# Sample maxima, exponentials and turned probabilities of a woven attention, in halves over several slots

## The chip, the cores and the metric

One Trainium2 chip, one core. The metric is the device time of one execution in microseconds (us), the median of the runs. A profile is one further execution with the hardware profiler on; times in it count from the start of its span.

## The reference, cut to what matters

One decoder layer is run for a prompt of 1024 tokens and for 8 sample sequences ("batches") of 4 new tokens each, which also attend to 4096 past tokens in a paged cache of keys and values (32 pages of 128 tokens for each batch, 8 heads of 64). After the attention come cross attention and a layer of 32 experts. The part that matters here:

```python
sp = jnp.einsum('bqhd,bkhd->bhqk', q, k_past) * scale + d_new[:, :, :, None] + rev[:, :, None, :]
sn = jnp.einsum('bqhd,bkhd->bhqk', q, k) * scale + d_new[:, :, :, None] - d_new[:, :, None, :]
p = jax.nn.softmax(jnp.concatenate([sp, where(causal, sn, -inf)], axis=-1), axis=-1)
out = p[..., :n_past] @ v_past + p[..., n_past:] @ v
```

So for each batch a score over all 4096 past tokens and the 4 new ones, its maximum, the exponentials, and the weighing of the values. The prompt has the same kind of attention among its own 1024 tokens.

## The kernel before

The attention of the samples and that of the prompt are woven into one list of 74 **slots** (n = 0 to 73; NSU = 64, LAG = 10, SU = 8 slots for a batch). Every engine walks the same list in its own loop (PE L1306, ACT L1908, DVE L2375) and they meet through semaphores, so the order within a slot is written out by hand for each engine. A slot n of the samples stands for 4 pages.

- **Keys.** SP loads 4 pages of keys (1 MB) into one of two buffers `kraw` (L928). It may refill a half of a buffer only when DVE has turned the keys that lay in it. DVE turns the keys of slot n + 2 in slot n (`turn_keys`, L2222, two transposes, L2230).
- **Scores.** PE makes the scores of slot n (L1270), ACT copies them out (`copy_scores`), PE sorts those of slot n - 1 (L1279), and DVE adds the decay `rev`, writes them into `sprob` of the batch and keeps a running maximum (`join_scores`, L2339).
- **The batch's softmax.** When the 8 slots of batch b are joined, which is in slot 8(b + 1), DVE finishes the maximum over the four page groups (L2351, L2354, eight small reduces inside `join_scores`) and signals `s_max`. ACT's `exp_pages` (L1888), last in ACT's slot 8(b + 1), takes the exponentials of both halves of `sprob` and of the new scores. In slot 8(b + 1) + 1 DVE's `turn_sample_probs` (L2357) turns all 1024 columns into `sprobT` (L2363) and the new ones into `pnewT` (L2364), and signals `st_ready`. There is one `sprobT` for all batches, so DVE first waits until PE has used up the batch before (`v_used`), the last of whose pages PE weighs at the end of that very slot 8(b + 1) + 1.
- **Values.** PE weighs the 4 pages of values of slot n - 10 at the end of slot n (`weigh_pages`, L1282, matmuls L1290; the batch's last page is followed by its new tokens, L1294). After a batch's last page DVE masks and sums the result (`mask_own`, L2366). POOL loads the values (`load_values`, L871, DMA at L876) into two buffers. The last ten loads (n = 54 to 63) also use places that the attention has done with (L258): place 4 is free when the last scores are joined, and place 5, which is the memory of the two `sprob`, when `st_ready` says that all of them are turned (L869). The odd ones of these ten are issued by SP (L994), in this order in its queue: values 55, 57, 59 (place 5), 61, the weights `c0` of the next stage (2 MB), values 63, and then the transformed input `xnT` from `xn_d` (L1000, 2 MB), without which the next stage's matmuls (L1338) don't start.
- **The prompt.** From slot 29 to 71 each slot holds one or two half units of the prompt's attention: PE's scores of the next unit (L1218, L1224), DVE's `biased` (L2301, with the maximum, L2312 and L2317), ACT's `exp_prompt` (L1880), PE's turning of the probabilities (L1232), ACT's copies of them (`probT`, L1830), PE's weighing (L1245) and the sums through `diag` (DVE L2328, PE L1249). Up to slot 28 there are projections of the prompt in their place (L1167, L1182).
- `spread_queries` (L2213, L2217) lays out the queries of the next batch; DVE does it in slot 8k ahead of everything but `join_scores`. PE needs it in slot 8(k + 1).

DVE's order in a slot is: `join_scores` of n - 1 (with the end of the maximum), `spread_queries`, the prompt's work, `turn_sample_probs`, `turn_keys`, `mask_own`. Below, "slot 8k" is one with n divisible by 8; slots 8k to 8k + 3 are called the four behind a batch's end, the other four the quiet ones.

Of the kernel before, what the change touches and what calls it, by code (L numbers as in the profile page):

```python
# [18 lines left out]
ALU = mybir.AluOpType  # L19
ACT = mybir.ActivationFunctionType  # L20
AX = mybir.AxisListType.X
# [6 lines left out]
DB, DS = 8, 4  # L28
# [8 lines left out]
QH = DS * H  # L37
# [108 lines left out]
def build_program(nc, t):  # L146

    ctx = ExitStack()
    with ctx:
# [100 lines left out]
        SU = PAGES // 4  # L250
# [608 lines left out]
        def values_free(eng, n):  # L859

            place = value_place(n)
            if values_in(n):
                eng.wait_ge(v_used, max(m for m in range(n) if value_place(m) == place) + 1)
            elif place in (2, 3):
                eng.wait_ge(kt_ready, 2 * (NSU - 3 + place))
            elif place == 4:
                R.read(eng, "sp", NSU - 1)
            elif place == 5:
                eng.wait_ge(st_ready, DB)  # L869

        def load_values(eng, n):  # L871

# [260 lines left out]
        def _(pe):  # L1133
# [148 lines left out]
            def weigh_pages(n):  # L1282

                b, u = n // SU, n % SU
                pe.wait_ge(v_in[value_place(n)], 64 * values_in(n) + 64)
                pe.wait_ge(st_ready, b + 1)
                if u == 0:
                    R.pe_free(pe, "so", b)
                for j in range(4):
                    last = nc.tensor.matmul(bank(6)[j * QH:(j + 1) * QH, :], sprobT[:, u, j * QH:(j + 1) * QH],  # L1290
                                            vpage[value_place(n)][:, j, :], start=u == 0, stop=u == SU - 1 and j > 0)
                last.then_inc(v_used, 1)
                if u == SU - 1:
                    nc.tensor.matmul(bank(6)[0:QH, :], pnewT[b % 2], vtok[0:NS, PT, :], start=False, stop=True  # L1294
                                     ).then_inc(R.full, 1)
# [531 lines left out]
        def _(act):  # L1827
# [57 lines left out]
                    copy(("pt", k, p, g), probT[p][:, j0:j0 + nj, :],  # L1885
                         lambda b: b[:, 0:nj * P].rearrange("p (j x) -> p j x", j=nj))

            def exp_pages(b):  # L1888
                act.wait_ge(s_max, b + 1)
                act.wait_ge(side_ready, SNEW_READY)  # L1890
                for r in range(2):
                    x = sprob[b % 2][:, r * 512:(r + 1) * 512]
                    nc.scalar.activation(x, x, ACT.Exp, bias=negmax[:, b:b + 1], accum_out=sums[:, b, r:r + 1]
                                         ).then_inc(s_exp, 1)
                nc.scalar.activation(pnew[b % 2], snew[:, b, :], ACT.Exp, bias=negmax[0:QH, b:b + 1],
                                     accum_out=sums[0:QH, b, 2:3]).then_inc(s_exp, 1)

# [10 lines left out]
            for n in range(NSU + LAG):  # L1908
                if n < NSU:
                    copy_scores(n)  # L1910
                if n == PROMPT0 - 1:
                    exp_prompt(0, 0)
                for k, p in halves(n):
                    if p == 0:
                        exp_prompt(k, 1)
                    copy_turned(k, p)
                    if p == 1 and k + 1 < NU:
                        exp_prompt(k + 1, 0)
                for item in items(n):
                    copy_item(*item)  # L1920
                if KOUT0 <= n < KOUT0 + TILES:
                    copy_key_rows(n - KOUT0)
                if SU <= n < NSU + SU and n % SU == 0:
                    exp_pages(n // SU - 1)
            def keep_first(name, f, q, after, kept=kept_c):

                if after is not None:
# [235 lines left out]
        def _(dve):  # L2163
# [49 lines left out]
            def spread_queries(b):  # L2213

                for g in range(4):
                    rows = slice(g * 32, (g + 1) * 32)
                    nc.vector.tensor_copy(  # L2217
                        qblk[b % 2].rearrange("p e (x q g) -> p e x q g", x=3, g=4)[rows, :, 0:3:2, :, g],
                        qgrp[rows, :, :, :, b * DS:(b + 1) * DS].rearrange("p j e x q -> p (j e) x q"))
                dve.drain()  # L2220

            def turn_keys(n):  # L2222

                if n >= NSU:
                    return
                dve.wait_ge(k_in[n % 2], 64 * (n // 2 + 1))
                if n >= 2:
                    R.made(dve, "sq", n - 2)
                for x in range(2):
                    nc.vector.transpose(kt[n % 2].rearrange("p c e s -> p (c e s)")[:, x * 1024:(x + 1) * 1024],  # L2230
                                        kraw[n % 2].rearrange("p c d -> p (c d)")[:, x * 1024:(x + 1) * 1024]
                                        ).then_inc(kt_ready, 1)
# [51 lines left out]
            def take_new():  # L2284

                dve.wait_ge(neg_stored, 32)
                nc.vector.tensor_tensor(nbias, consts[0:QH, C_MASK:C_MASK + DB * NS].rearrange("p (b s) -> p b s", b=DB),
                                        nd.unsqueeze(1).to_broadcast([QH, DB, NS]), ALU.add)
                dve.drain()
                R.made(dve, "snew")  # L2290
                nc.vector.tensor_tensor(snew, bank(R.bank("snew"))[0:QH, 0:DB * NS].rearrange("p (b s) -> p b s", b=DB), nbias,
                                        ALU.add).then_inc(R.by["dve"], 1)
                dve.drain()
                nc.vector.tensor_reduce(tops[0:QH, :, SU:SU + 1], snew, AX, ALU.max).then_inc(side_ready, 1)
                R.made(dve, "lf")
                b = bank(R.bank("lf"))
                nc.vector.tensor_copy(lfo[:, 0:PT, :], b[:, 0:PT * H].rearrange("p (i h) -> p i h", i=PT))
                nc.vector.tensor_copy(lfo[0:NS, PT, :], b[0:NS, PT * H:TILES * H]).then_inc(R.by["dve"], 1)
                dve.drain()
# [39 lines left out]
            def join_scores(n):  # L2339

                b, u = n // SU, n % SU
                if u == 0:
                    dve.wait_ge(rev_in[b % 2], 16 * (b // 2 + 1))
                R.made(dve, "sp", n)
                nc.vector.tensor_tensor_reduce(out=sprob[b % 2][:, u * PAGE:(u + 1) * PAGE], in0=bank(3)[:, 0:PAGE],
                                               in1=rev[b % 2][:, u * PAGE:(u + 1) * PAGE], scale=1.0, scalar=-3e38,
                                               op0=ALU.add, op1=ALU.max, accum_out=tops[:, b, u:u + 1]).then_inc(R.by["dve"], 1)
                if u == SU - 1:
                    dve.drain()
                    for g in range(4):  # L2350
                        nc.vector.tensor_reduce(crest[:, g:g + 1], tops[g * QH:(g + 1) * QH, b, :], AX, ALU.max)  # L2351
                    dve.drain()
                    for g in range(4):
                        last = nc.vector.tensor_reduce(negmax[g * QH:(g + 1) * QH, b:b + 1], crest, AX, ALU.max, negate=True)  # L2354
                    last.then_inc(s_max, 1)

            def turn_sample_probs(b):  # L2357

                dve.wait_ge(s_exp, 3 * b + 3)
                if b:  # L2360
                    dve.wait_ge(v_used, b * SU)
                flat = sprobT.rearrange("p u x -> p (u x)")
                nc.vector.transpose(flat, sprob[b % 2])  # L2363
                nc.vector.transpose(pnewT[b % 2], pnew[b % 2]).then_inc(st_ready, 1)  # L2364

            def mask_own(b):  # L2366

# [7 lines left out]
            for n in range(NSU + LAG):  # L2375
                if 0 < n <= NSU:
                    join_scores(n - 1)
                if n % SU == 0 and n + SU < NSU:
                    spread_queries(n // SU + 1)
                if n == PROMPT0 - 1:  # L2380
                    biased(0, 0)
                if n == END:
                    take_prompt(NU - 1)
                if n < 3:
                    take_forget(n)
                for k, p in halves(n):
                    if p == 0 and k:
                        take_prompt(k - 1)
                    if k + 1 < NU and p < len(chunks(k + 1)):
                        biased(k + 1, p)  # L2390
                    if p == 1:
                        invert_sums(k)
                if n == 5:
                    take_new()
                if SU < n < NSU + SU and n % SU == 1:
                    turn_sample_probs(n // SU - 1)
                turn_keys(n + 2)
                if 2 * SU < n < NSU + LAG - 1 and n % SU == 1:
                    mask_own(n // SU - 2)
            near, far = slice(0, HT), slice(HT, NT)  # L2400
# [919 lines left out]
```

## Time and profile before

| what | value |
|---|---|
| median of 3 runs | 2012.65 us (2010.44 to 2016.42) |
| the profiled execution: its own time, its span | 2018.6 us, 2016.9 us |
| busy: PE, DVE, ACT, POOL | 1876.5, 861.9, 440.3, 249.4 us |
| DMA | 458.57 MB, mean 227 GB/s |
| chain that ended last | PE 82%, DVE 6%, ACT 4%, DMA 4%, issue 3% |
| slots 0 to 28 | 70.9 to 273.0 us |
| slots 29 to 73 | 273.0 to 547.2 us, then the next stage |

How to read it: PE is the busiest engine, but it is busy through matmuls that wait on others in some stages. The woven attention is the part of the span from 71 to 547 us. What a change in it is worth is what it moves the instant at which the next stage's first matmul (L1338) starts.

### The profile page before, as it was taken

Reading aid. Unit: us, or ns where it says so; the run is one execution under the profiler, and the core shown is the slowest. Engines: PE = TensorE matmul, PEld = TensorE weight load, DVE = VectorE, ACT = ScalarE, POOL = GpSimd, SP = SyncE. Lnnn points to the kernel's source line nnn. Section 1 sums busy time; section 2 is a strip of 40 time slices with the busy share of each in tenths; the row PEclk is TensorE's granted clock in tenths of the full one; section 3 lists DMA queues with packets and bytes.
Section 4 is the critical chain, followed back from the end, with each engine's and each line's share of the span. In section 5 each row is a group of like instructions: output and inputs, shape, how many; then the busy total and the mean of one; then the engine's idle time right before and its main releaser. Section 6 shows DMA issues by size and latency. Waiting matters only on the chain.

```text
span 2016.9 us, 33708 instructions
## 1 busy us (share of the span) xinstructions
PE 1876.5 (93%) x12473; PEld 1121.2 (56%) x12473; DVE 861.9 (43%) x1921; ACT 440.3 (22%) x1017; POOL 249.4 (12%) x381
## 2 busy tenths in 40 slices
PE   6999998888999999999999998987999999999994
PEld 4677655555488868888874487444333333333331
DVE  5644467777656523333344647245111111111115
ACT  3111124444301011101110305131222222212213
POOL 0203333333100000000000000000111111111110
PEclk9999999999999999999999999996999999999997
DMA  7859999999911140210121205344999999999966
GB/s 255 277 169 343 354 337 364 352 339 347 331 63 65 44 154 11 63 53 11 55 74 63 87 1 183 121 171 177 372 381 382 374 373 376 371 372 374 371 222 264
DMA packets 208164, 458.57 MB, mean 227 GB/s; under 512 B 18721, under 2 KB 47418, under 8 KB 207618
## 3 DMA queue, kind: packets, MB, share of 16 engines
q1 hardware_dynamic: 177554, 365.30, 50.8%
q0 software_dynamic: 30448, 91.13, 12.8%
q8 instruction: 100, 1.64, 0.3%
q14 instruction: 62, 0.51, 0.1%
HBM read 432.44 MB, written 32.17 MB: 230 GB/s over the span
## 4 chain that ended last, share of the span: by engine, by line
PE 82%; DVE 6%; ACT 4%; DMA 4%; issue 3%; DVEq 1%; SPq 0%; ACTq 0%; POOLq 0%; POOL 0%
PE ps L1338 20%; PE ps L1691 11%; PE ps L1722 6%; PE ps L1167 6%; PE ps L1403 6%; PE ps L1702 6%; PE ps L1432 5%; PE ps L1731 3%; PE ps L1182 3%; PE ps L1544 2%; PE ps L1290 2%; PE ps L1270 2%; PE ps L1148 1%; DVE kt L2230 1%; DMA vpage<-in_cache_v 1%
## 5 line engine op out<-in xcount | busy, mean ns | idle before, releaser
L1691 PE MATMUL ps<-gu,xgT 128*64 128x512 f32 x1024 | 228.7, 599 | 0.6 <-ACT xgT L2046 0.6
L1338 PE MATMUL ps<-xnT,ring 128*128 128x264 f32 x768 | 184.5, 392 | 3.2 <-ACT xnT L741 1.9
L2230 DVE STREAM_TRANSPOSE kt<-kraw 128x1024 f32<-128x1024 f32 x128 | 151.1, 1219 | 34.5 <-DMA kraw<-in_cache_k 25.3
L1338 PEld LDWEIGHTS ps<-xnT,ring 128*128 128x128 f32 x768 | 147.8, 193 | 30.5 <-ACT xnT L741 2.2
L876 POOL DMA_DIRECT2D vpage<-in_cache_v x228 | 122.4, 537 | 291.6 <-PE ps L1290 233.6
L3053 DVE TENSOR_TENSOR sig_a<-ps,sig_a 128x256 f32<-128x256 f32 x32 | 13.6, 425 | 322.9 <-ACT sig_a L2050 322.9
L1691 PEld LDWEIGHTS ps<-gu,xgT 128*64 128x64 f32 x1024 | 71.1, 138 | 133.0 <-issue 130.2
L1722 PE MATMUL ps<-wd,hidT_a 128*64 128x512 f32 x512 | 116.9, 598 | 20.2 <-ACT hidT_a L2056 11.2
L1702 PE MATMUL ps<-gu,xgT 128*32 128x512 f32 x1024 | 115.8, 592 | 0.0
L1167 PE MATMUL ps<-xnT,early 128*128 128x352 f32 x320 | 101.2, 472 | 4.4 <-DVE xnT L2174 4.4
L1167 PEld LDWEIGHTS ps<-xnT,early 128*128 128x128 f32 x320 | 60.6, 194 | 38.2 <-issue 8.7
L1270 PEld LDWEIGHTS ps<-kt,qblk 128*32 128x32 f32 x2048 | 58.2, 112 | 40.6 <-issue 37.9
L1722 PEld LDWEIGHTS ps<-wd,hidT_a 128*64 128x64 f32 x512 | 37.2, 136 | 77.7 <-issue 60.6
L1955 ACT ACTIVATE gate<-gate 128x264 f32<-128x264 f32 x64 | 27.0, 423 | 234.8 <-DVE gate L2599 234.8
L3187 POOL DMA_DIRECT2D x_d<-xs x5 | 2.7, 539 | 599.4 <-DVE xs L756 599.4
L1702 PEld LDWEIGHTS ps<-gu,xgT 128*32 128x32 f32 x1024 | 33.1, 110 | 77.0 <-issue 77.0
L1290 PE MATMUL ps<-vpage,sprobT 128*32 128x512 f32 x480 | 66.4, 625 | 7.4 <-DMA vpage<-in_cache_v 7.4
L1270 PE MATMUL ps<-kt,qblk 128*32 128x128 f32 x2048 | 69.9, 277 | 0.9 <-DVE kt L2230 0.9
L1182 PE MATMUL ps<-early,xnT 128*128 128x256 f32 (+1 forms) x288 | 66.0, 384 | 0.0
L2590 DVE TENSOR_TENSOR gate<-ps,gate 128x264 f32<-128x264 f32 x64 | 27.7, 433 | 82.9 <-PE ps L1403 82.9
L1731 PE MATMUL ps<-wd,hidT_b 128*32 128x512 f32 x512 | 61.6, 598 | 1.3 <-ACT hidT_b L2065 1.3
L1403 PE MATMUL ps<-cyT,upw 128*128 128x264 f32 x256 | 62.2, 386 | 0.0
(482 smaller groups left out, 2945.9 us busy)
## 6 DMA issues: line engine op xcount, KB each, us to landing
kraw<-in_cache_k SPq DMA_DIRECT2D x256, 256.0 KB, 5.3
wd<-in_w_expert_down SPq DMA_DIRECT2D x31, 2048.0 KB, 21.5
gu<-in_w_expert_gate SPq DMA_DIRECT2D x30, 2048.0 KB, 20.3
gu<-in_w_expert_up SPq DMA_DIRECT2D x30, 2048.0 KB, 25.1
vpage<-in_cache_v POOLq DMA_DIRECT2D x228, 256.0 KB, 5.8
ring<-in_w_in SPq DMA_DIRECT2D x12, 1024.0 KB, 8.1
yy<-y_d SPq DMA_DIRECT2D x16, 512.0 KB, 10.4
early<-in_w_in SPq DMA_DIRECT2D x6, 1024.0 KB, 11.7
```

Of the source, the lines that this page charges most:

```text
L876: eng.dma_start(vpage[value_place(n)][:, p, :], t["cache_v"][ds(page, 1)].rearrange("a s d -> (a s) d")).then_inc(v_in[value_place(n)], 16)
L1167: last = nc.tensor.matmul(bank(R.bank(name, f, n))[:, 0:NC_], weight[:, k, :], xnT[:, k, cols_of(n)], start=k == 0, stop=k == KD - 1)
L1182: last = nc.tensor.matmul(bank(R.bank(kind, a, b))[0:r, 0:256], xnT[:, k, b * P:b * P + r], early[a][:, k, :], start=k == 0, stop=k == KD - 1)
L1270: last = nc.tensor.matmul(bank(5)[j * 32:(j + 1) * 32, 0:PAGE], qblk[b % 2][:, 2 * j + x % 2, first:first + 32], kt[n % 2][:, :, 4 * j + x ...
L1290: last = nc.tensor.matmul(bank(6)[j * QH:(j + 1) * QH, :], sprobT[:, u, j * QH:(j + 1) * QH], vpage[value_place(n)][:, j, :], start=u == 0 ...
L1338: last = nc.tensor.matmul(bank(R.bank(name, f, q))[:, 0:QT], weight[:, k], src[:, k, cols], start=k == 0, stop=k == HK - 1)
L1403: last = nc.tensor.matmul(bank(R.bank(name, f, q, half))[:, 0:QT], upw[f % 2][:, x, k, :], src[:, k, quarter(half, q)], start=k == 0, stop ...
L1691: last = nc.tensor.matmul(bank(0)[h * BA:(h + 1) * BA, :].rearrange("p (x n) -> p x n", x=2), src[:, k, 0:BA], weight[:, k, :, h * DE // 2 ...
L1702: last = nc.tensor.matmul(bank(1)[c:c + BB, :].rearrange("p (x n) -> p x n", x=2), src[:, k + odd, BA:BLK], weight[:, k + odd, :, h * DE / ...
L1722: last = nc.tensor.matmul(bank(6)[o * BA:(o + 1) * BA, :], hidT_a[:, c % 2, c // 2 * BA:(c // 2 + 1) * BA], weight[:, c, o * 512:(o + 1) * ...
L1731: last = nc.tensor.matmul(bank(7)[q:q + BB, :], hidT_b[:, odd, c // 2 * BB:(c // 2 + 1) * BB], weight[:, c + odd, o * 512:(o + 1) * 512], ...
L2230: nc.vector.transpose(kt[n % 2].rearrange("p c e s -> p (c e s)")[:, x * 1024:(x + 1) * 1024], kraw[n % 2].rearrange("p c d -> p (c d)")[: ...
```

## The change

The end of the maximum becomes a step of its own (`join_tops`) and is put behind the prompt's work in slot 8k. ACT takes the exponentials of the first half of `sprob` in slot 8k and those of the second half and of the new scores in slot 8k + 1. DVE turns the first half in slot 8k + 1, behind `turn_keys`, waiting for PE to be through with only the first four pages' places of the batch before, and the second half with `pnewT` in slot 8k + 3. `st_ready` counts halves, PE's weighing and the load into place 5 wait on the new counts. `spread_queries` goes to the end of slot 8k + 4.

```diff
--- before.py
+++ after.py
@@ -866,7 +866,7 @@
             elif place == 4:
                 R.read(eng, "sp", NSU - 1)
             elif place == 5:
-                eng.wait_ge(st_ready, DB)
+                eng.wait_ge(st_ready, 2 * DB)
 
         def load_values(eng, n):
 
@@ -1283,7 +1283,7 @@
 
                 b, u = n // SU, n % SU
                 pe.wait_ge(v_in[value_place(n)], 64 * values_in(n) + 64)
-                pe.wait_ge(st_ready, b + 1)
+                pe.wait_ge(st_ready, 2 * b + 1 + u // (SU // 2))
                 if u == 0:
                     R.pe_free(pe, "so", b)
                 for j in range(4):
@@ -1885,13 +1885,14 @@
                     copy(("pt", k, p, g), probT[p][:, j0:j0 + nj, :],
                          lambda b: b[:, 0:nj * P].rearrange("p (j x) -> p j x", j=nj))
 
-            def exp_pages(b):
+            def exp_pages(b, r):
                 act.wait_ge(s_max, b + 1)
+                x = sprob[b % 2][:, r * 512:(r + 1) * 512]
+                nc.scalar.activation(x, x, ACT.Exp, bias=negmax[:, b:b + 1], accum_out=sums[:, b, r:r + 1]
+                                     ).then_inc(s_exp, 1)
+
+            def exp_new(b):
                 act.wait_ge(side_ready, SNEW_READY)
-                for r in range(2):
-                    x = sprob[b % 2][:, r * 512:(r + 1) * 512]
-                    nc.scalar.activation(x, x, ACT.Exp, bias=negmax[:, b:b + 1], accum_out=sums[:, b, r:r + 1]
-                                         ).then_inc(s_exp, 1)
                 nc.scalar.activation(pnew[b % 2], snew[:, b, :], ACT.Exp, bias=negmax[0:QH, b:b + 1],
                                      accum_out=sums[0:QH, b, 2:3]).then_inc(s_exp, 1)
 
@@ -1921,7 +1922,9 @@
                 if KOUT0 <= n < KOUT0 + TILES:
                     copy_key_rows(n - KOUT0)
                 if SU <= n < NSU + SU and n % SU == 0:
-                    exp_pages(n // SU - 1)
+                    exp_pages(n // SU - 1, 0)
+                if SU <= n < NSU + SU and n % SU == 1:
+                    exp_pages(n // SU - 1, 1), exp_new(n // SU - 1)
             def keep_first(name, f, q, after, kept=kept_c):
 
                 if after is not None:
@@ -2345,23 +2348,27 @@
                 nc.vector.tensor_tensor_reduce(out=sprob[b % 2][:, u * PAGE:(u + 1) * PAGE], in0=bank(3)[:, 0:PAGE],
                                                in1=rev[b % 2][:, u * PAGE:(u + 1) * PAGE], scale=1.0, scalar=-3e38,
                                                op0=ALU.add, op1=ALU.max, accum_out=tops[:, b, u:u + 1]).then_inc(R.by["dve"], 1)
-                if u == SU - 1:
-                    dve.drain()
-                    for g in range(4):
-                        nc.vector.tensor_reduce(crest[:, g:g + 1], tops[g * QH:(g + 1) * QH, b, :], AX, ALU.max)
-                    dve.drain()
-                    for g in range(4):
-                        last = nc.vector.tensor_reduce(negmax[g * QH:(g + 1) * QH, b:b + 1], crest, AX, ALU.max, negate=True)
-                    last.then_inc(s_max, 1)
-
-            def turn_sample_probs(b):
-
-                dve.wait_ge(s_exp, 3 * b + 3)
+
+            def join_tops(b):
+
+                dve.drain()
+                for g in range(4):
+                    nc.vector.tensor_reduce(crest[:, g:g + 1], tops[g * QH:(g + 1) * QH, b, :], AX, ALU.max)
+                dve.drain()
+                for g in range(4):
+                    last = nc.vector.tensor_reduce(negmax[g * QH:(g + 1) * QH, b:b + 1], crest, AX, ALU.max, negate=True)
+                last.then_inc(s_max, 1)
+
+            def turn_sample_probs(b, r):
+
+                dve.wait_ge(s_exp, 3 * b + (1, 3)[r])
                 if b:
-                    dve.wait_ge(v_used, b * SU)
-                flat = sprobT.rearrange("p u x -> p (u x)")
-                nc.vector.transpose(flat, sprob[b % 2])
-                nc.vector.transpose(pnewT[b % 2], pnew[b % 2]).then_inc(st_ready, 1)
+                    dve.wait_ge(v_used, b * SU - (SU // 2, 0)[r])
+                half = slice(r * 512, (r + 1) * 512)
+                last = nc.vector.transpose(sprobT.rearrange("p u x -> p (u x)")[:, half], sprob[b % 2][:, half])
+                if r == 1:
+                    last = nc.vector.transpose(pnewT[b % 2], pnew[b % 2])
+                last.then_inc(st_ready, 1)
 
             def mask_own(b):
 
@@ -2375,8 +2382,6 @@
             for n in range(NSU + LAG):
                 if 0 < n <= NSU:
                     join_scores(n - 1)
-                if n % SU == 0 and n + SU < NSU:
-                    spread_queries(n // SU + 1)
                 if n == PROMPT0 - 1:
                     biased(0, 0)
                 if n == END:
@@ -2392,9 +2397,15 @@
                         invert_sums(k)
                 if n == 5:
                     take_new()
+                if 0 < n <= NSU and n % SU == 0:
+                    join_tops(n // SU - 1)
+                turn_keys(n + 2)
                 if SU < n < NSU + SU and n % SU == 1:
-                    turn_sample_probs(n // SU - 1)
-                turn_keys(n + 2)
+                    turn_sample_probs(n // SU - 1, 0)
+                if SU < n < NSU + SU and n % SU == 3:
+                    turn_sample_probs(n // SU - 1, 1)
+                if n % SU == 4 and n + SU < NSU:
+                    spread_queries(n // SU + 1)
                 if 2 * SU < n < NSU + LAG - 1 and n % SU == 1:
                     mask_own(n // SU - 2)
             near, far = slice(0, HT), slice(HT, NT)
```

## Rows read from the trace of the kernel before

**Rows 1.** Stretch: us, busy PE, PEld, DVE, ACT, POOL, clock, DMA share, GB/s

```profile
157.00:268.00 111.00, 110.35 (x1096) 71.96 (x1094) 54.51 (x100) 14.95 (x46) 36.53 (x68) 1.00 1.00 354
```

**Rows 2.** The same view, slots 32 to 63 in stretches of four slots

```profile
294.77:326.35 31.58, 26.10 (x331) 15.93 (x327) 24.97 (x72) 14.44 (x35) 10.72 (x20) 0.95 0.94 328
326.35:350.92 24.57, 21.88 (x326) 14.64 (x322) 16.82 (x50) 10.36 (x28) 10.69 (x20) 1.00 1.02 373
350.92:381.11 30.19, 23.98 (x312) 13.98 (x307) 25.80 (x73) 12.38 (x31) 8.60 (x16) 0.94 0.99 363
381.11:404.07 22.96, 21.71 (x321) 14.07 (x317) 16.66 (x49) 9.94 (x25) 8.59 (x16) 1.00 0.97 341
404.07:432.65 28.58, 24.00 (x302) 14.02 (x298) 23.92 (x72) 11.20 (x31) 8.59 (x16) 0.88 0.90 309
432.65:458.22 25.57, 22.46 (x325) 14.18 (x321) 17.67 (x49) 9.72 (x25) 8.58 (x16) 1.00 1.03 378
458.22:484.03 25.81, 22.15 (x319) 13.75 (x314) 22.89 (x70) 11.85 (x31) 8.58 (x16) 1.00 0.97 334
484.03:507.55 23.52, 20.99 (x309) 13.34 (x305) 15.33 (x46) 8.97 (x25) 9.33 (x18) 1.00 1.00 365
```

**Rows 3.** DVE in order of time, slots 48 and 49

```profile
406.59 0.64 DVE L2351 TENSOR_REDUCE crest<-tops 32x1 f32<-32x9 f32 x4
...
407.98 0.93 DVE L2217 COPY qblk<-qgrp 32x64 f32<-32x64 f32 x4
409.02 0.29 DVE L2312 CUSTOM_DVE_ANT_0 prob<-ps,negk 128x128 f32<-128x128 f32 x1
...
416.39 1.25 DVE L2363 STREAM_TRANSPOSE sprobT<-sprob 128x1024 f32<-128x1024 f32 x1 [1.64 <-PE ps L1290]
```

**Rows 4.** Lines L2363 and L2364: durations min/median/max ns, first and last start; idle before

```profile
L2363 DVE STREAM_TRANSPOSE sprobT<-sprob x8: 1245/1246/1246, 148.1 to 517.7; 128x1024 f32<-128x1024 f32 x8
...
  PE ps L1290: 19.7, 7
...
L2364 DVE STREAM_TRANSPOSE pnewT<-pnew x8: 156/156/157, 149.3 to 518.9; 32x32 f32<-32x32 f32 x8
```

**Rows 5.** ACT in order of time, around the exponentials in slot 32

```profile
302.35 0.71 ACT L1893 ACTIVATE sprob<-sprob,negmax 128x512 f32<-128x512 f32 x1
...
304.22 1.03 ACT L1880 ACTIVATE prob<-prob,fstat 128x896 f32<-128x896 f32 x1
```

**Rows 6.** PE in order of time: some of its waits of slots 30 to 65

```profile
289.91 1.97 PE L1245 MATMUL ps<-probT,vtok 128*64 128x128 f32 x32 [0.94 <-ACT probT L1830]
...
301.48 0.44 PE L1249 MATMUL ps<-diag,onesw 128*64 128x128 f32 x4 [1.03 <-DVE diag L2328]
...
305.96 1.73 PE L1232 MATMUL ps<-consts,prob 128*128 128x128 f32 x7 [2.21 <-ACT probT L1830]
...
515.62 0.96 PE L1232 MATMUL ps<-consts,prob 128*128 128x128 f32 x7 [1.22 <-ACT probT L1830]
```

**Rows 7.** Waits of SP's queue from 500 to 560 us: total, times, longest

```profile
SPq L876 <- DVE pnewT L2364: 6.4, 1, 6.4
```

**Rows 8.** SP's queue in order of time, end of the attention

```profile
508.50 12.60 SPq L876 DMA_DIRECT2D vpage<-in_cache_v  x8
523.51 1.88 SPq L876 DMA_DIRECT2D kraw<-in_cache_v  x4
525.44 1.44 SPq L825 DMA_DIRECT2D ring<-in_w_in  x2
529.27 2.56 SPq L876 DMA_DIRECT2D vpage<-in_cache_v  x4
536.16 0.81 SPq L1000 DMA_DIRECT2D xnT<-xn_d  x2
```

**Rows 9.** In order of time: DVE in slot 67, PE at the attention's end

```profile
528.66 0.15 DVE L2317 TENSOR_REDUCE fstat<-ftop 128x2 f32<-128x2 f32 x1
...
544.92 1.04 PE L1294 MATMUL ps<-vtok,pnewT 32*32 32x512 f32 x2
547.21 2.03 PE L1338 MATMUL ps<-xnT,ring 128*128 128x264 f32 x6 [1.25 <-DMA xnT<-xn_d]
```

## The prediction

> **What bounds the kernel now.** I read the stretches first, because the page's shares mix stages. From 157 to 268 us, slots 11 to 27, PE is busy for 110.4 of 111.0 us [rows 1]. Up to there DVE and ACT may wait as they like; PE does not. So the change can give nothing ahead of slot 29, and the edits in those slots cost nothing either, as long as PE's 100% covers them. If that cover were gone, DVE's wait for PE's last page there (part of the 19.7 us of rows 4) would be the first to show.
>
> From slot 29 on it is different. The reader should see in rows 2 that the stretches come in two kinds. The four slots behind a batch's end (first, third, fifth and seventh row) take 31.6, 30.2, 28.6 and 25.8 us, together 116.2. The four quiet ones take 24.6, 23.0, 25.6 and 23.5, together 96.6. The difference is 19.5 us, of which 1.0 each is work (the new tokens' matmul, one such as the 1.04 us of L1294 in rows 9); 15.5 us is what batch ends cost on top. In the same stretches the clock that PE was granted sinks to 0.95, 0.94, 0.88 and the DMA rate is 334 GB/s (38.8 MB in 116.2 us) against 365 (35.2 MB in 96.6 us). No engine is full there. The bound is the round between PE, ACT and DVE for each prompt unit, with the transfers close behind it.
>
> **Part 1, DVE's order in slot 8k.** Today the eight reduces (0.64 us for four of them, so 1.3) and `spread_queries` (0.93) stand ahead of `biased`: it starts at 409.02, and could at 406.6 [rows 3]. That is 2.3 us off the way from the prompt's scores to their maximum, to ACT's exponential and to `diag`. Price of it on PE: the wait for `diag` in slot 33 is 1.03 us [rows 6], and is the largest of three in slots 8k + 1 (the others 0.2 and 0.7). I take 1.9 us in all. What is late next: `s_max`, now behind `invert_sums`. ACT reaches the exponentials only after its copies and the next unit's exponential, about 1.5 to 3 us after the prompt's maximum, so I cost it at nothing; without that cover it is 1.3 us in each of five slots.
>
> **Part 2, ACT.** The block of exponentials occupies ACT from 302.35 to 304.2 [rows 5], and `exp_prompt` of the next half unit stands behind it. Halved, 0.7 us stays in slot 8k and about 1.0 goes to the end of slot 8k + 1, where ACT has nothing queued until PE's next scores. PE waits for ACT's `probT` once in each slot 8k + 1: five waits, the first 2.21 and the last 1.22 us, together 8.8 [rows 6]. Such a wait in a quiet slot is 0.94 [rows 6], since the turning of a half unit with two groups always waits for a copy. The parts 1 and 2 together take these five down to that: 8.8 - 5 x 0.9 = 4.3 us.
>
> **Part 3, DVE's wait for PE.** DVE stands 19.7 us, in seven waits, for the batch before to be used up [rows 4], and `turn_keys`, `mask_own` and the next slot's joins are queued behind it. The new waits ask for pages that were weighed three slots earlier, so they are free. `mask_own` still waits for the same instant, but with neither L2363's 1.25 us nor the keys left behind it. As a gain on PE it is already in the 4.3 us, and it lets keys be refilled some us earlier, which raises the DMA rate in the slow stretches.
>
> **Part 4, the transposes.** One of 1024 columns is 1.25 us, one of 32 is 0.16 [rows 4]; on that line 512 columns are 0.68. Two are 0.12 us more than the one, at least 0 and at most 1.25 (two full ones). They and `spread_queries` now lie in slots 8k + 3 and 8k + 4, which were quiet: 0.8 and 0.9 us of DVE. DVE is busy for 17 of 25 us there; I charge a quarter, 0.3 us on each of four, 1.2 us.
>
> **Part 5, the clock.** One minus the clock, times the length, is 1.6, 1.8 and 3.4 us in the slow stretches [rows 2]: 6.8 us of PE's work lost, each right behind PE's longest waits. With waits of 0.9 I expect half of it back where PE paces, and take 2.0; ends 0 and 6.8. Sum of the middle: 1.9 + 4.3 + 2.0 - 1.2 = **7 us gained**, against 15.5 at the very most.
>
> A check by bytes: if the slow stretches ran at the quiet ones' 365 GB/s, their 38.8 MB would take 106.2 us, 10 us less. So 7 is not barred by the transfers as rows 2 show them. The Trainium skill, DMA: Bandwidth & Descriptors, section Specifications, gives a limit of about 358 GB/s for one core on the memory. By it the 74 MB of slots 32 to 63 need 206.7 of their 212.8 us, and the gain could be 6 us at most. The trace disagrees: 373 and 378 GB/s over some 25 us each [rows 2].
>
> **Part 6, the end: a wait that grows.** Place 5 of the values is the memory of `sprob`, and its load (values 59) now waits for the second half of the last batch, turned in slot 67 and not in 65. SP already waits 6.4 us for `pnewT` [rows 7], which is ready at 519.0 [rows 4]. In slot 67 the prompt's maximum is done at 528.8 [rows 9], then 0.68 and 0.16 us of transposes: ready at 529.6, **10.6 us later** (DVE idles behind it, so they cost DVE nothing). In SP's queue stand, behind this load, values 61, the weights `c0`, values 63 and `xnT`. From 519.0 to the end of the issue of values 63 at 531.8 SP takes 12.8 us [rows 8]; now that ends at 542.4. `xnT` was issued at 536.16 [rows 8], because it waited for the prompt's last scores, so 4.3 us of the delay are hidden and 6.2 are not. It lands 11 us after its issue, and PE waits for exactly that landing (547.21, [rows 9]). Values 59 are weighed at about 536, which a load issued at 529.6 to 531.6 just reaches; values 63 come late, but inside the wait for `xnT`. Ends: the landing may take fewer than 11 us; alone, 2.2 MB at 375 GB/s are 6 us, which leaves 1 us; the other end is 10.6. By bytes: from 529.6 on six megabytes of values and weights and 2.2 of `xnT`, 8.5 MB at 365 GB/s, end at 552.8, 5.6 us late. I take **5.5 us lost**.
>
> **Sum.** -7 + 5.5 = -1.5; everything behind 547 us only shifts. Against the profiled execution's own 2018.6 that is 2017.1. It lies 6.0 us above the median of the runs, 2012.65, so the forecast in runs is 2011.1. A measurement can tell about 0.3% (6 us) here, so this is "no change".
>
> **Rivals.**
> Rival 1, faster: the batch ends give most of what they hold, 12 of the 15.5 us (the keys are refilled earlier, the clock stays up), and the end costs 2, since `xnT` lands on idle DMA engines. Then -10, 2002.6. For it: DVE's 19.7 us of waiting, the full 10 us by bytes. Against it: the DMA share is 0.94 to 1.02 in most of rows 2. Chance 0.28.
> Rival 2, slower: one mechanism, SP's queue at the end. The price is up to the full 10.6 us if values 59 and 61 are late for their own slots and `c0` for DVE's sums of it, with `xnT` behind them. It decides from the point where the second half is ready more than 4.3 us after 519.0. With 3 us gained before it: +7.6, 2020.2. For it: rows 7 and 8, PE has only 1.25 us of idle time before `xnT` lands. Against it: latency falls when the queues are empty. Chance 0.17.
> Rival 3, the pages are the bound: slots 32 to 63 can't run faster than the 354 GB/s that rows 1 hold for 111 us. 74 MB are then 209 us, a gain of 3.7, less the end's 5.5: +1.8, 2014.5. The page on DMA named above would be its rule. Chance 0.15.
> The change not doing what it says: DVE waits at `mask_own` as it did at the transpose. That falls under rival 3's time.
>
> **Numbers.** Forecast 0.40, rivals 0.28, 0.17, 0.15. Faster by over 0.3%: most of rival 1 and a sixth of the forecast, 0.32. Slower: most of rival 2 and a little of the others, 0.19. The rest, 0.49, is the same. The range goes from rival 1 to rival 2, 2001 to 2021; the forecast's own is 2006 to 2016.
>
> **What would show it.** Right: no wait of DVE for L1290 ahead of L2363; the stretches of slots 32 to 35, 40 to 43 and 48 to 51 shorter by some 2 us each with the clock near 1.00; ACT's block halved; SP's wait for `pnewT` up from 6.4 to some 17 us; `xnT` issued later than the prompt's last scores and PE idle for over 5 us before L1338. Wrong: PE idle before L1338 still about 1 us; the four-slot stretches unchanged; ACT waiting for `s_max`; or PE waiting for values 59.

## The result, and the profile after

The changed kernel is slower: a median of 2023.2 us (2017.0 to 2026.7, 14 runs) against 2013.4 for the kernel before (2009.8 to 2019.9, 14 runs) in the same series. The ratio is 1.0039, 95% interval 1.0029 to 1.0050, so 5.8 to 10.1 us. The forecast was 1.5 us faster, with 2021 us as the upper end.

First the stretches of four slots in the changed kernel, the counterpart of [rows 2], then its last stretch, from slot 64 to the first matmul of the next stage. The columns are those of [rows 1].

```profile
291.66:327.53 35.87, 27.36 (x334) 16.25 (x330) 25.07 (x69) 14.58 (x35) 10.76 (x20) 0.86 0.91 336
327.53:351.60 24.07, 21.75 (x329) 14.60 (x325) 16.48 (x52) 10.33 (x28) 10.76 (x20) 1.00 0.95 330
351.60:379.50 27.90, 23.64 (x313) 14.30 (x309) 23.65 (x69) 12.62 (x31) 8.62 (x16) 0.94 1.01 376
379.50:403.10 23.60, 21.74 (x325) 14.11 (x321) 19.64 (x56) 9.95 (x25) 8.63 (x16) 1.00 0.98 360
403.10:430.20 27.10, 22.55 (x302) 13.72 (x298) 23.08 (x68) 11.55 (x31) 8.61 (x16) 0.94 1.01 374
430.20:453.50 23.30, 21.94 (x325) 14.29 (x321) 18.18 (x55) 9.61 (x25) 8.61 (x16) 1.00 1.00 363
453.50:478.30 24.80, 21.76 (x322) 13.50 (x317) 22.22 (x69) 12.22 (x31) 8.61 (x16) 1.00 0.95 340
...
502.98:550.94 47.96, 37.03 (x318) 17.43 (x310) 26.07 (x90) 17.80 (x43) 6.46 (x12) 0.91 0.78 279
```

From slot 40 on the stretches behind a batch's end are 1.0 to 2.3 us shorter each, as forecast; in the second profile of the same kernel (after_again) the one of slots 40 to 43 is not, with 31.7 us. The first one is 4.3 us longer. And the last one lasts 48.0 us where the kernel before takes 39.7. The same columns for that stretch in the kernel before, then for its two parts in the changed kernel, up to the issue of values 59 and from there on:

```profile
507.55:547.21 39.66, 34.98 (x318) 17.51 (x311) 22.81 (x84) 17.68 (x43) 7.84 (x15) 1.00 0.99 344
```

```profile
502.98:524.70 21.72, 19.04 (x172) 9.56 (x167) 14.35 (x58) 11.34 (x28) 4.30 (x8) 1.00 0.53 196
524.70:550.94 26.24, 18.00 (x151) 7.87 (x150) 11.72 (x33) 6.47 (x16) 2.15 (x4) 0.83 0.98 347
```

In the first part the DMA engines are busy for about half of the time (0.53). SP's queue in order of time shows why; the rows answer to [rows 8] and [rows 7].

```profile
503.93 1.90 SPq L876 DMA_DIRECT2D vpage<-in_cache_v  x4
524.72 1.89 SPq L876 DMA_DIRECT2D vpage<-in_cache_v  x4
529.01 2.00 SPq L876 DMA_DIRECT2D kraw<-in_cache_v  x4
531.05 1.45 SPq L825 DMA_DIRECT2D ring<-in_w_in  x2
534.91 3.57 SPq L876 DMA_DIRECT2D vpage<-in_cache_v  x4
538.58 0.86 SPq L1000 DMA_DIRECT2D xnT<-xn_d  x2
```

```profile
SPq L876 <- DVE pnewT L2370: 16.5, 1, 16.5
```

Values 57 go out at 503.9, then SP stands 16.5 us (before: 6.4) until the last batch's second half is turned; values 59 follow at 524.7. PE in order of time, the counterpart of [rows 9]:

```profile
538.82 1.06 PE L1290 MATMUL ps<-vpage,sprobT 128*32 128x512 f32 x8
545.80 1.94 PE L1290 MATMUL ps<-vpage,sprobT 128*32 128x512 f32 x8 [5.91 <-DMA vpage<-in_cache_v]
547.66 1.91 PE L1294 MATMUL ps<-vtok,pnewT 32*32 32x512 f32 x2
550.94 9.71 PE L1338 MATMUL ps<-xnT,ring 128*128 128x264 f32 x32 [1.37 <-DMA xnT<-xn_d]
```

PE idles 5.9 us for values 63 and 1.4 for `xnT`, and right after the idle time the same eight matmuls take 1.94 us instead of 1.06: the granted clock is 0.60 on the mean from 539.9 to 550.9 us.

A second profile of the kernel before showed how far one profile may be trusted, so I compare durations within the span, of all profiles taken. Each ratio is to the kernel before in the same series; a version had 12 runs there (the changed kernel 14 in its first series, the last two of the table 6). All in us, from PE's first score matmul of slot 29, its sort of slot 64 and its first L1338:

```
kernel            slots 29-63   64 to next stage   ratio to before, 95% interval
before               234.5          39.7            -
before_again         233.1          39.5            (one run)
gate_alone           232.0          47.9            1.0040  1.0025-1.0054
before_c0            232.8          39.5            1.0004  0.9992-1.0016
bias_later_only      236.8          40.2            1.0002  0.9987-1.0016
changed kernel       231.4          48.0            1.0039  1.0029-1.0050
after_again          231.2          48.1            1.0031  1.0016-1.0045
last_whole           229.9          39.9            0.9996  0.9983-1.0009
c0_ahead             228.2          43.0            1.0000  0.9988-1.0012
both_ends            234.2          40.3            0.9994  0.9982-1.0006
tops_ahead           233.9          38.7            0.9985  0.9970-1.0001
keys_ahead           226.5          39.8            0.9971  0.9958-0.9984
keys_tops_behind     229.7          40.7            0.9992  0.9978-1.0006
keys_bias            227.7          40.2            0.9973  0.9959-0.9986
bias_later           230.4          39.0            0.9982  0.9968-0.9997
bias_later_tops      225.9          39.1            0.9953  0.9937-0.9969
best_again           226.6          39.1            0.9953  0.9936-0.9970
```

Kernels with the middle of before (first five rows) take 233.8 us on the mean for slots 29 to 63, those with the changed middle (next five) 231.0. With a scatter of about 2 us from profile to profile the 2.8 are uncertain by more than 1 us. The end is 8.4 us longer and hardly scatters. So -2.8 + 8.4 = +5.6 us, to be held against the 6.2 and 7.9 of the two series.

### The profile page after: what moved, and what is told of

Read it like the earlier page. It is cut to its first block, busy times and chain, and to the rows that moved or that the text cites. A ratio compares the mean times of both kernels' runs of the same rounds, so it can differ in the third digit from the quotient of the medians.

```text
span 2018.1 us, 33715 instructions
## 1 busy us (share of the span) xinstructions
PE 1872.8 (93%) x12473; PEld 1119.7 (55%) x12473; DVE 861.5 (43%) x1929; ACT 442.1 (22%) x1017; POOL 250.3 (12%) x381
## 4 chain that ended last, share of the span: by engine, by line
PE 81%; DVE 5%; DMA 4%; issue 4%; ACT 3%; DVEq 1%; SPq 1%; POOLq 0%; POOL 0%; ACTq 0%
PE ps L1338 20%; PE ps L1691 11%; PE ps L1722 6%; PE ps L1167 6%; PE ps L1403 6%; PE ps L1702 6%; PE ps L1432 5%; PE ps L1182 3%; PE ps L1731 3%; PE ps L1544 3%; PE ps L1270 2%; PE ps L1290 2%; DMA vpage<-in_cache_v 2%; PE ps L1148 1%; PE ps L1218 1%
## 5 line engine op out<-in xcount | busy, mean ns | idle before, releaser
L1338 PE MATMUL ps<-xnT,ring 128*128 128x264 f32 x768 | 183.4, 390 | 3.3 <-ACT xnT L741 1.9
L1338 PEld LDWEIGHTS ps<-xnT,ring 128*128 128x128 f32 x768 | 147.1, 192 | 31.1 <-DMA xnT<-xn_d 3.1
L1830 ACT ACTIVATE probT<-ps 128x512 f32<-128x512 f32 (+3 forms) x96 | 43.7, 488 | 85.9 <-PE ps L1232 85.9
```

Of the source, the lines that this page charges most:

```text
L1338: last = nc.tensor.matmul(bank(R.bank(name, f, q))[:, 0:QT], weight[:, k], src[:, k, cols], start=k == 0, stop=k == HK - 1)
```

## The experiments

### The end

**The changed kernel again** (after_again), no edit.

> The changed kernel once more, for a second profile and a second timing. Theory Q (the queue at the end: the load into place 5 waits for the second half, and the input of the next stage stands behind it): 6 to 10 us over the kernel before; SP's wait for pnewT 15 to 20 us, PE idle 5 to 8 us in all before L1338. Rival M (the middle: DVE stands longer at the keys in slots 29 to 63, as for the 5.6 us in slot 35 of the first profile): the same total, but slot 64 is reached no earlier than the 507.6 us of the kernel before. Rival K (no gain anywhere, the early slots lose): slot 29 later than 273 us.

1.0031; SP waits 16.5 us for `pnewT`, PE waits 5.5 us for values 63 and 1.4 for `xnT`. Theory Q's picture to the row. Slot 64 came at 503.5, so rival M doesn't hold the loss; slot 29 came at 272.2, so K doesn't either.

**The last batch turned whole** (last_whole).

```diff
-                if SU <= n < NSU + SU and n % SU == 1:
+                if n == NSU or (SU <= n < NSU and n % SU == 1):
                     exp_pages(n // SU - 1, 1), exp_new(n // SU - 1)
...
-                if SU < n < NSU + SU and n % SU == 3:
+                if n == NSU + 1 or (SU < n < NSU and n % SU == 3):
                     turn_sample_probs(n // SU - 1, 1)
```

> The changed kernel, with the last batch's two halves both exponentiated in slot 64 and turned in slot 65, so that the load into place 5 is free as early as before. Theory Q: 7 to 9 us faster than the changed kernel, so 0 to 5 us faster than the kernel before; PE idle before L1338 back to 1 to 2 us. Rival M: within 2 us of the changed kernel, since the middle is untouched. Rival K: the same as M.

0.9996: 7 us come back from one batch of eight. SP waits 6.5 us for `pnewT`, the end takes 39.9 us.

**The delay alone, in the kernel before** (gate_alone).

```diff
             elif place == 5:
                 eng.wait_ge(st_ready, DB)
+                R.read(eng, "ps", NU - 2, 0, 1)
```

> The kernel before, unchanged but for one more wait: SP's load into place 5 also waits for DVE's maximum of the half unit in slot 67, about 9.5 us later than pnewT. The delay alone. Theory Q: 6 to 9 us slower than the kernel before, with 5 to 8 us of PE idle time before L1338. Rival M: 0 to 2 us slower.

1.0040. One wait on SP, nothing else, costs as much as the whole change. PE in order of time in that kernel (one line further down in the file):

```profile
547.63 1.94 PE L1291 MATMUL ps<-vpage,sprobT 128*32 128x512 f32 x8 [5.62 <-DMA vpage<-in_cache_v]
549.50 1.91 PE L1295 MATMUL ps<-vtok,pnewT 32*32 32x512 f32 x2
552.78 7.47 PE L1339 MATMUL ps<-xnT,ring 128*128 128x264 f32 x20 [1.37 <-DMA xnT<-xn_d]
```

Counted from slot 64, these are the rows of the changed kernel to 0.1 us, and PE's wait for values 63 to 0.3. The price of the end is shown from both sides: taken away in last_whole, and put in here alone.

**c0 ahead of values 59** (c0_ahead; in the kernel before, before_c0; with last_whole, both_ends).

```diff
-                if n == NSU - 3:
+                if n == NSU - 7:
                     ring_load(sp, "c0")
```

> The changed kernel, with the 2 MB of weights c0 issued ahead of values 59 (behind values 57), so that they move while SP would stand. The wait of SP for the second half stays. Theory Q with the price in bytes behind the wait (8.5 MB less 2.1): 4 to 6 us faster than the changed kernel. Theory Q with the price in SP's issues alone: some 1.5 us faster (the issue of c0 is 1.4 us). Rival M: within 1 us of the changed kernel.

1.0000, and the end takes 43.0 us: five of the eight are back, more than the 1.4 us of issue. `xnT` goes out 3.0 us earlier, since the issue of values 63 is also short again (1.9 us, not 3.6), and it lands 10.4 us after its issue, not 12.4. So SP's own time for c0 is the smaller part of the five; the rest is that fewer bytes are left to move behind the wait. That the short issue comes from that too is likely, not shown. Of the eight us, what is left is a wait of 4.4 us for `xnT`, issued 32.6 us behind the start of slot 64 (28.6 in the kernel before).

> The kernel before, with the weights c0 issued ahead of values 59. There SP stands only 6.4 us for pnewT. Theory Q: the end is bound by what stands in SP's queue and by bytes, so 1 to 4 us faster than the kernel before, since xnT lands earlier and PE's wait ahead of L1338 (1.25 us) goes. Rival E (PE's own work ends the attention there): within 1 us. Slot 64 as in the other profile of before: 506 to 508 us under theory S, 502 to 504 under rival T.

> The changed kernel with the last batch turned whole in slot 65 and with c0 ahead of values 59. Theory S with Q: 4 to 7 us faster than the kernel before, no PE wait of over 1 us ahead of L1338. Rival T: as before_c0, so 1 to 4 us faster than the kernel before.

1.0004 and 0.9994. Where SP isn't stopped for long, c0's place is worth nothing. The wait ahead of L1338 did vanish in before_c0, but sixteen matmuls later, at 548.2, PE waits 0.3 us for `xnT` all the same, and the end takes 39.5 us, as in the kernel before (39.5 and 39.7). My 1 to 4 us were wrong, rival E was right.

**The kernel before, a second profile** (before_again).

> The kernel before, for a second profile of its middle: its first profile was of a run 4 to 5 us above its median. Theory S (the change gains 4 us in slots 29 to 63 and loses 8 behind them): slot 64 is reached at 506 to 508 us, as in the first profile (507.6), against 503 in the changed kernel's two. Rival T (the middle gains nothing, the first profile of before was a slow one): 502 to 504 us.

Slot 64 came at 505.3, between the two theories. The other profiles of that middle gave 504.5 to 508.8, of the changed one 499.3 to 506.5. The changed middle probably gains something, but less than my first pair of profiles said.

### The middle

**Maxima and queries back ahead of the prompt** (tops_ahead: last_whole with `join_tops` and `spread_queries` where the kernel before has them).

> As last_whole, but with the end of the maximum and the layout of the next queries back ahead of the prompt's work in slot 8k: what is left of the change is the halved exponentials, the halved transposes and the keys ahead of them. If part 1 of the prediction (2.3 us off the prompt's way) is worth its 1.9 us: 1 to 3 us slower than last_whole, and PE waits for diag L2328's counterpart by 0.2 to 1 us in slots 33, 49 and 57. Rival (the transfers take back what the middle gives): within 1 us of last_whole.

0.9985, 0.1% faster than last_whole, not slower. PE's waits for `diag` did come back, with 1.0 and 0.9 us in slots 33 and 49, so the gain forecast by part 1 is there, and something else in the move costs as much. Alone the intervals overlap. So the end of the maximum was moved by itself.

**The keys first, nothing else** (keys_ahead), and that with the end of the maximum behind the prompt's work (keys_tops_behind).

```diff
+                turn_keys(n + 2)
                 if SU < n < NSU + SU and n % SU == 1:
                     turn_sample_probs(n // SU - 1)
-                turn_keys(n + 2)
```

> The kernel before, with only DVE's turn_keys put ahead of the turning of the sample's probabilities in slots 8k + 1: no halves, maxima and queries as they were. If the gain of tops_ahead comes from the keys no longer standing behind DVE's wait for PE: 1 to 4 us faster than the kernel before and the late keys near 310 us show up here too. If it comes from the halved exponentials: within 1 us of the kernel before, and no such wait.

> keys_ahead with only the end of the maximum moved behind the prompt's work of slot 8k. The prediction's part 1: 1 to 3 us faster than keys_ahead, so 0.9955 to 0.9967 of the kernel before. Theory P (that move is what spoils last_whole against tops_ahead): 2 to 5 us slower than keys_ahead, so 0.998 to 1.0.

0.9971 and 0.9992: two lines swapped in the kernel before give 6 us, and the moved maximum takes 4 of them back (the two intervals overlap by 0.0006; last_whole against tops_ahead and bias_later against bias_later_tops point the same way). The two come from different series, each against its own kernel before. Of the late keys near 310 us a wait of 1.2 us shows up in keys_ahead; PE's 2 us waits for ACT in slots 8k + 1 are still there; that they give the transfers their time is my reading, and wasn't tried. In the waits of keys_tops_behind from 200 to 530 us (total, times, longest), and in ACT's order of time in slot 48, stands a wait that the kernel before doesn't have:

```profile
ACT sprob L1893 <- DVE negmax L2357: 4.6, 5, 1.2
```

```profile
404.15 0.83 ACT L1880 ACTIVATE prob<-prob,fstat 128x640 f32<-128x640 f32 x1 [1.22 <-DVE fstat L2317]
...
406.23 0.72 ACT L1893 ACTIVATE sprob<-sprob,negmax 128x512 f32<-128x512 f32 x1 [1.16 <-DVE negmax L2357]
```

ACT gets the prompt's maximum 1.0 us earlier, counted from the start of slot 49, and then stands 1.16 us at the sample's. That alone is 0.2 to 0.3 us. But PE's wait for `probT` in the slot behind is 2.83 us there and 1.95 in keys_ahead, and its matmuls behind the longer wait run slower. PE in slot 49 of keys_tops_behind:

```profile
409.65 1.01 PE L1232 MATMUL ps<-consts,prob 128*128 128x128 f32 x5 [2.83 <-ACT probT L1830]
410.59 1.94 PE L1290 MATMUL ps<-vpage,sprobT 128*32 128x512 f32 x8
```

In keys_ahead the same groups take 0.74 and 1.07 us, and slot 49 as a whole 8.9 us instead of 10.8. The columns of [rows 1] for slots 29 to 63, keys_ahead first, then keys_tops_behind:

```profile
272.63:499.13 226.50, 195.08 (x2748) 122.47 (x2744) 177.98 (x512) 97.54 (x253) 81.00 (x152) 0.99 0.99 359
```

```profile
272.14:501.88 229.74, 200.03 (x2749) 124.73 (x2745) 178.06 (x512) 98.01 (x253) 82.08 (x153) 0.96 0.98 356
```

The granted clock is 0.96 instead of 0.99, and PE is busy 5 us longer with the same matmuls. Between these two profiles the clock lost behind longer waits of PE covers the 3.2 us of difference; another such wait is for values at the end of slot 40, 3.7 us against 2.4. It isn't the whole account: keys_bias, which also has the maximum in its old place, takes 227.7 us at 0.97. The changed kernel has the same wait of ACT for `negmax`, four times in its slots 29 to 63:

```profile
ACT sprob L1891 <- DVE negmax L2359: 3.5, 4, 1.2
```

**The late keys.** In the changed kernel DVE, in order of time in slot 34, and PE in slot 35:

```profile
309.16 0.69 DVE L2315 CUSTOM_DVE_ANT_0 prob<-ps,negk 128x512 f32<-128x512 f32 x1
...
316.42 2.37 DVE L2233 STREAM_TRANSPOSE kt<-kraw 128x1024 f32<-128x1024 f32 x2 [6.56 <-DMA kraw<-in_cache_k]
...
320.07 0.48 DVE L2331 TENSOR_SCALAR diag<-consts,fstat 128x128 f32<-128x128 f32 x2
```

```profile
314.14 0.88 PE L1245 MATMUL ps<-probT,vtok 128*64 128x128 f32 x12 [0.63 <-ACT probT L1830]
320.61 0.70 PE L1249 MATMUL ps<-diag,onesw 128*64 128x128 f32 x4 [5.59 <-DVE diag L2331]
```

The whole prompt work of slot 35 is queued behind the keys. The stretches of the changed kernel around it, in the columns of [rows 1]:

```profile
300.00:318.00 18.00, 12.89 (x173) 7.95 (x173) 10.47 (x27) 6.35 (x17) 5.86 (x11) 0.96 1.03 397
318.00:330.00 12.00, 8.66 (x74) 4.78 (x74) 8.54 (x28) 4.34 (x10) 1.41 (x3) 0.63 0.70 227
```

In the first the DMA engines move 397 GB/s (353 in the first profile of the kernel before in the same stretch, 363 to 391 in three others of that middle), and the keys, issued up to 301.0, need 15 us; in the second there is nothing to move, since PE hasn't freed the values' buffers. All five profiles of the changed middle have this wait, with 4.9 to 5.7 us on PE.

**negk later**, the 1 MB that DVE's `biased` adds to the prompt's scores (bias_later: last_whole; bias_later_only: the kernel before; bias_later_tops and best_again: tops_ahead; keys_bias: keys_ahead).

```diff
-                if n == 35:
+                if n == 37:
                     R.made(sp, "k", 3, 1)
                     sp.wait_ge(xn_stored, 16)
                     load_negk(1)
```

> As last_whole, but the load of 1 MB of negk for the second pair of heads stands two key loads later in SP's queue (behind keys 37, not keys 35). Theory W (in the changed kernels the keys of slot 36 land late because too much is in flight from 295 us on, and DVE stands at them): DVE's wait at the keys near 310 us falls from 6.5 to under 2 us, PE's 5.7 us wait for diag in slot 35 goes, slots 32 to 35 fall from 34 to 31 us, and the time is 1 to 4 us under last_whole's. Rival V (the keys are late by their own issue, after the turning of the keys before): the wait stays at 4 to 6 us and the time within 1 us of last_whole.

0.9982; the stretch of slots 32 to 35 went from 34.9 to 27.3 us, but that of 36 to 39 from 24.1 to 31.6: DVE stands 5.58 us at keys there. The wait moved to the next slots' keys; theory W is half right, since too much in flight did cause it in slot 35, but there is more of it behind.

> The kernel before with the same move of negk and nothing else. Theory W: there DVE is itself late, so the keys are not waited for: within 1 us of the kernel before. Rival: 1 to 3 us faster, and the move is a gain of its own.

1.0002, as W said.

> tops_ahead with the same move of negk. Theory W: 3 to 7 us faster than the kernel before, the best of all. If it isn't below tops_ahead's 0.9985 of the kernel before, the transfers take back elsewhere what slot 35 gives.

0.9953, twice (best_again: 0.9953, median 2005.2 against 2014.5), with intervals that end at 0.9969 and 0.9970, where tops_ahead's begins. Against bias_later, of the same series, it is some 6 us faster, and all that differs is the place of the maxima and queries. Here slots 32 to 35 take 28.2 us and 36 to 39 25.7 and 24.1; DVE's longest wait at the keys there is 3.8 and 1.9 us. This version beats both kernels, by 9 us and some 16.

> keys_ahead (the kernel before with turn_keys first in slots 8k + 1) with negk two key loads later, nothing halved. If the halves are worth something beside the order of the keys: slower than bias_later_tops' 0.9953 of the kernel before by 2 us or more, so 0.996 to 0.998, with PE's waits of 2 us for ACT's probT in slots 8k + 1 still there. If they are worth nothing: 0.995 to 0.996.

0.9973, the same as keys_ahead. So without the halves the move of negk gives nothing, and with them the kernel is 0.2% faster than without; since the intervals overlap a little, the halves' own 4 us are likely, not shown.

> The same kernel as bias_later_tops, once more, since that had only 6 runs: 0.994 to 0.997 of the kernel before; slot 64 reached at 496 to 501 us.

## Why the prediction was wrong

The forecast was 1.5 us gained, the median says 7.9 lost (the changed kernel's second series 6.2), and 2023.2 lies above the range's 2021. Two terms of the sum failed. The end was priced at 5.5 and cost 8.4, 2.9 us of the miss. The larger part is the middle: 7 forecast, 2.8 in the profiles, and less than 1 by the ratio of last_whole, which has the changed middle without the longer wait at the end (0.9996, 0.9983 to 1.0009). That alone would have made "no change"; what made the kernel slower is the end.

**Part 6 was the right mechanism with too small a size.** The second half was ready 10.1 us later behind slot 64 (10.6 forecast), and SP's queue with `xnT` behind it came as written; the term was 5.5 and measured 8.4. `xnT` was issued 35.6 us behind slot 64 against 28.6 [rows 8], so 7.0 later (I had 6.2), since the issue of values 63 took 3.6 us instead of 2.6. It landed 12.4 us after its issue where the kernel before has 11 and I had taken less: I took a discount for empty DMA engines, but the bytes that hadn't moved while SP stood (a share of 0.53 over those 21.7 us) were in its way. 7.0 and 1.3 are the 8.4, to 0.1. Values 63, "late, but inside the wait for `xnT`", came at 545.8, and that held: PE still waits for `xnT` last, so neither the 5.9 us of waiting nor the half rate behind it is added to that instant. The bound from bytes gave 5.6 and agreed with my choice only because it took 365 GB/s from values 59 on, where the trace has 347 over 26.2 us (236 over the first six). Rival 2 had the place; its +7.6 is nearly the total, from an end of 10.6 that was too high and 3 us gained before it. I gave it 0.17, because I treated the end as a size and not as what decides.

**Part 1, "I cost it at nothing".** The cover I named for the later `s_max`, ACT's copies and exponential, isn't there: ACT waits five times for `negmax`, 4.5 us in all. "ACT waiting for `s_max`" was one of my own signs of being wrong. I had written down the price without that cover (1.3 us in each of five slots) and then left it out. The gain on the other side was real: the three `diag` waits of slots 8k + 1 are gone. Net, the move costs about 4 us (keys_tops_behind against keys_ahead), and some 6 together with the queries (bias_later against bias_later_tops).

**Part 2 held as a wait.** PE's five waits for `probT` in slots 8k + 1 fell from 8.8 to 3.9 us (0.63, 0.34, 0.74, 0.56 and 1.62), 4.9 us where 4.3 were forecast. That is the wait, and not time gained: keys_ahead still has most of these waits and isn't slower than tops_ahead, which has them reduced (0.9971 and 0.9985).

**Part 3 had the wrong sign at its end.** Keys refilled earlier do raise the DMA rate near 310 us, 397 to 401 GB/s in three profiles of the changed middle against 353 to 391. But DVE now comes to them before they have landed, and 6.6 us of standing at the keys replace what it had waited for PE. That one wait takes 5.6 us from PE in slot 35, most of the 7 forecast for the middle. "What is late next" should have been asked of DVE's own next instruction.

**Part 5** returned nothing where 2.0 us were forecast: 5.0, 1.7, 1.6 and 0 us of lost clock in the four stretches, 8.3 in all against 6.8. The clock is lowest, 0.86, in the stretch with PE's longest idle time, the 5.6 us, and that only changed its place. **Part 4** held in the price of a transpose, 0.67 us for 512 columns against 0.68; the 1.2 us charged on PE were not tried by themselves. Of the bytes: the limit of about 358 GB/s for one core that the prediction cites from the Trainium skill (DMA: Bandwidth & Descriptors, section Specifications) is again passed here, with 376 and 374 GB/s over two stretches of 27 us, and slots 29 to 63 of bias_later_tops as a whole run at 362. Rival 3's cap of 354 falls with it.

## What to carry to other kernels

When a step is moved later, look up every wait on its signal on the DMA queues too, and price all that stands behind the stopped queue until the next stage's first input: here an in-order queue that waited 10 us longer cost 8.4 of them, and 2 MB sent ahead of the wait gave five back. Order an engine's list by who is waiting, as these runs suggest: a signal that another engine needs at once (the maximum) goes early, work that waits for another engine goes behind work that doesn't. And undo parts one by one after a change of many parts: here one swap of two lines gave 6 us in the kernel before, and one of the other parts took most of that back.

## What the runs showed that I had not expected

The waits of a closed round replace each other. Removing PE's 2.2 us for ACT brought 5.6 us at the keys, moving 1 MB of loads out of the way brought 5.6 us at the next slots' keys, and only with the maximum back in its place did the longest wait there shrink to 3.8 and 1.9 us. Yet the same 1 MB moved in kernels without the halves changed nothing (1.0002, 0.9973 against 0.9971). A second point: profiles of the same middle differ by up to 6 us in slots 29 to 63 (228.2 to 234.2), in part by whether DVE stands 2.5 to 2.9 us at the keys near 370 us and PE 3.4 to 3.8 us for `diag` behind it, or neither does, so one pair of profiles can't give the size of a gain of 3.
